# Dilated logits over 128 rows, with query halves moved by DMA, first steps a quarter of a unit later, and token factors spread by transposes

## The reference

```python
for g, (window, dil) in enumerate(((128, 1), (512, 4), (2048, 16))):
    s = einsum('bnqrhc,bnkrhc->bnrhqk', qb, kc) * HEAD_DIM ** -0.5    # 8 heads of 64
    logits = where(valid, s + bias, NEG_INF)
    m = max(logits); p = exp(logits - m); den = sum(p)
    num = einsum('bnrhqk,bnkrhc->bnqrhc', p, vc)
o = sum(num * exp(m - m_all)) / sum(den * exp(m - m_all))
```

## Time and profile before

| | us |
|---|---|
| median of 3 runs | 1864.54 (1863.68 to 1864.83) |
| the profiled execution | 1863.83 |
| its span | 1862.1 |
| TensorE busy | 1850.5 (99%) |
| VectorE busy | 1127.5 (61%) |
| ScalarE busy | 672.8 (36%) |
| GpSimd busy | 165.3 (9%) |

### The profile page before, as it was taken

One profiled execution on the slowest core, in us unless ns is written; L12 is line 12 of the kernel. 1 busy time (PEld: TensorE's weight loads), 2 busy tenths in 40 slices (PEclk: granted clock), 3 DMA queues, 4 the chain that ended last, 5 costly groups with the idle time before them and its releaser, 6 DMA issues.

```text
span 1862.1 us, 24221 instructions
## 1 busy us (share of the span) xinstructions
PE 1850.5 (99%) x8817; PEld 1535.1 (82%) x8817; DVE 1127.5 (61%) x1524; ACT 672.8 (36%) x975; POOL 165.3 (9%) x199
## 2 busy tenths in 40 slices
PE   9999999999999999999999999999999999999998
PEld 7888888888888888888888888888888878888887
DVE  7888788676676444686642354366776786325532
ACT  6323434343333333344321222225555653212221
POOL 0011112200000011002000000101211220000000
PEclk9999999999999999999999999999999999999999
DMA  4222222323233333223333343322222123333232
GB/s 161 81 89 80 80 68 80 113 91 101 90 101 94 109 103 125 84 75 93 119 101 93 115 121 97 104 93 71 78 69 80 47 90 113 102 93 100 90 102 68
DMA packets 55156, 175.29 MB, mean 94 GB/s; under 512 B 6201, under 2 KB 12857, under 8 KB 55074
## 3 DMA queue, kind: packets, MB, share of 16 engines
q1 hardware_dynamic: 49744, 170.43, 29.4%
q10 hardware_dynamic: 4818, 3.68, 0.9%
q0 software_dynamic: 512, 0.03, 0.0%
HBM read 171.96 MB, written 2.13 MB: 93 GB/s over the span
## 4 chain that ended last, share of the span: by engine, by line
PE 94%; DVE 5%; DMA 0%; issue 0%; ACT 0%; SPq 0%; DVEq 0%; ACTq 0%
PE ps L605 30%; PE ps L607 29%; PE ps L606 29%; PE ps L1101 1%; DVE wlo L1621 1%; PE ps L1132 1%; PE ps L1113 1%; PE ps L613 1%; PE ps L903 1%; PE ps L893 0%; DVE yr L1640 0%; DVE grm L1713 0%; PE ps L1144 0%; PE ps L980 0%; DVE h L2286 0%
## 5 line engine op out<-in xcount | busy, mean ns | idle before, releaser
L605 PE MATMUL ps<-xhi,whi 128*128 128x512 f32 x1568 | 617.2, 394 | 1.4 <-DVE wlo L1621 0.6
L607 PE MATMUL ps<-xlo,whi 128*128 128x512 f32 x1568 | 610.9, 390 | 0.0
L606 PE MATMUL ps<-xhi,wlo 128*128 128x512 f32 x1568 | 610.5, 389 | 0.0
L1621 DVE TENSOR_TENSOR wlo<-raw,whi 128x1024 fp32r<-128x1024 f32 x314 | 403.8, 1287 | 210.8 <-ACT whi L1257 210.6
L1257 ACT ACTIVATE whi<-raw 128x1024 fp32r<-128x1024 f32 x314 | 331.1, 1055 | 537.6 <-PE ps L607 475.4
L605 PEld LDWEIGHTS ps<-xhi,whi 128*128 128x128 f32 x1568 | 294.4, 188 | 64.9 <-DVE wlo L1621 1.9
L607 PEld LDWEIGHTS ps<-xlo,whi 128*128 128x128 f32 x1568 | 294.3, 188 | 62.0
L606 PEld LDWEIGHTS ps<-xhi,wlo 128*128 128x128 f32 x1568 | 294.6, 188 | 59.3
L605 PE MATMUL ps<-mh,whi 128*128 128x512 f32 (+1 forms) x528 | 202.2, 383 | 0.0
L606 PE MATMUL ps<-mh,wlo 128*128 128x512 f32 (+1 forms) x528 | 202.0, 383 | 0.0
L607 PE MATMUL ps<-mh,whi 128*128 128x512 f32 (+1 forms) x528 | 202.0, 383 | 0.0
(11 more groups left out here) (346 smaller groups left out, 1962.4 us busy)
## 6 DMA issues: line engine op xcount, KB each, us to landing
raw<-wst SPq DMA_DIRECT2D x314, 512.0 KB, 3.5
h<-xT SPq DMA_DIRECT2D x8, 256.0 KB, 5.6
out<-h SPq DMA_DIRECT2D x8, 256.0 KB, 2.2
raw<-wst SPq DMA_DIRECT2D x4, 256.0 KB, 5.4
bias_a<-bias_rows ACTq DMA_DIRECT2D x4, 256.0 KB, 4.6
bias_b<-bias_rows ACTq DMA_DIRECT2D x4, 256.0 KB, 4.4
wsf<-wsT ACTq DMA_DIRECT2D x1, 512.0 KB, 3.4
bsb<-bs ACTq DMA_DIRECT2D x1, 512.0 KB, 4.3
```

What stands on the lines that cost most here:

```text
L605: pe.matmul(o, w[0], x[0], start=first, stop=False, **kw)
L606: pe.matmul(o, w[1], x[0], start=False, stop=False, **kw)
L607: return pe.matmul(o, w[0], x[1], start=False, stop=done, **kw)
L1621: dve.tensor_tensor(wlo[:, n % SLOTS, :], raw[:, n % 2, :], whi[:, n % SLOTS, :].bitcast(F32), ALU.subtract).then_inc(s_split, 1)
```

## The change

The query and key parts of each group are laid out anew. `dqk[:, o, x]` holds, for head x, both halves of the query over 128 rows (high and low, one in each set of 64 rows), and `dqk[:, o, 2 + x]` holds the key's high part twice. One matmul over 128 rows then gives high by high plus low by high for a head; high by low (`dqk[:, o, 4]`) stays a pair over 64 rows. To lay this out, ScalarE copies the second head's high half within its rows (`head_halves`, at the second tick of the next unit), and issues two DMAs per q or k unit, 64 rows x 2 KB each, that move halves to the other rows; TensorE waits for the DMAs (`s_dqm`). Part 1 of the last pair keeps the old form. A burst now multiplies the 128-row products of both its steps first, then the 64-row ones. The steps of part 0 come one tick later, except the last two of pair 3, which keep theirs. The token factors are spread by transposes of the broadcast column.

```diff
--- before.py
+++ after.py
@@ -145,10 +145,11 @@
-    _d, _l = TICKS * (9 * _p + 6) - 1, TICKS * (9 * _p + 9)
+    _d, _l = TICKS * (9 * _p + 6), TICKS * (9 * _p + 9)
     for _s in range(4):
         _n = 8 * _p + _s
-        LOGITS_AT[_d + 3 * _s], TURN_AT[_d + 3 * _s + 2], SUMS_AT[_d + 3 * _s + 5] = _n, _n, _n
+        _t = _d + (3 * _s if _p < 3 else (0, 3, 5, 8)[_s])
+        LOGITS_AT[_t], TURN_AT[_t + 2], SUMS_AT[_t + 5] = _n, _n, _n
@@ -333,14 +334,15 @@
-            dqk = sb("dqk", [P, 3, 4, T], F32R, m)
+            dqk = sb("dqk", [P, 3, 5, T], F32R, m)
+            qlow = sb("qlow", [P, T], F32R, m)
...
+        def stacked(p, part):
+            return p < 3 or part == 0
+        def moves_before(p, o):
+            return 6 * p + 2 * o
...
@@ -962,8 +975,7 @@ spread()
-                        ins = pe.matmul(bank(7 - n)[:, t * P:(t + 1) * P], rtk[:, NT * n + t:NT * n + t + 1].to_broadcast([P, P]), ident,
-                                        start=t == 0, stop=True, skip_group_check=True)
+                        ins = pe.transpose(bank(7 - n)[:, t * P:(t + 1) * P], rtk[:, NT * n + t:NT * n + t + 1].to_broadcast([P, P]), ident)
@@ -1052,8 +1064,7 @@ last_spread(half)
-                    ins = pe.matmul(bank(6)[:, t * P:(t + 1) * P], rtok[:, t:t + 1].to_broadcast([P, P]), ident, start=t == tiles[0],
-                                    stop=True, skip_group_check=True)
+                    ins = pe.transpose(bank(6)[:, t * P:(t + 1) * P], rtok[:, t:t + 1].to_broadcast([P, P]), ident)
@@ -1082,25 +1093,47 @@
-            def logits(n):
+            def blocks_of(n):
...
-                for i, (o, q, k, c) in enumerate(blocks):
-                    for a, b in ((0, 2), (1, 2), (0, 3)):
-                        for x, r in enumerate(rows):
-                            ins = pe.matmul(logit_half(n)[:, x, c], dqk[r, o, a, q], dqk[r, o, b, k],
-                                            start=n % 2 == 0 and i == 0 and (a, b) == (0, 2), stop=b == 3, skip_group_check=True)
-                ins.then_inc(s_dlo, 1)
+            def logits(steps):
+                for n in steps:
+                    p, part, t = step_of(n)
+                    if n % 4 == 0:
+                        if stacked(p, part):
+                            pe.wait_ge(s_dqm, 32 * moves_before(p, 3 if part else 2))
+                        else:
+                            pe.wait_ge(s_dqk, 6 * p + 6)
+                    if n % 2 == 0 and n or n > PAIRED:
+                        pe.wait_ge(s_dlg, n)
+                for n in steps:
+                    p, part, t = step_of(n)
+                    for i, (o, q, k, c) in enumerate(blocks_of(n)):
+                        first = n % 2 == 0 and i == 0
+                        if stacked(p, part):
+                            for x in range(2):
+                                pe.matmul(logit_half(n)[:, x, c], dqk[:, o, x, q], dqk[:, o, 2 + x, k], start=first, stop=False,
+                                          skip_group_check=True)
+                        else:
+                            for qs in (dqk[:, o, 0, q], qlow[:, q]):
+                                for x, r in enumerate(HEAD_ROWS):
+                                    pe.matmul(logit_half(n)[:, x, c], qs[r, :], dqk[r, o, 2, k], start=first, stop=False,
+                                              skip_group_check=True)
+                                first = False
+                for n in steps:
+                    p, part, t = step_of(n)
+                    for o, q, k, c in blocks_of(n):
+                        for x, r in enumerate(HEAD_ROWS):
+                            ins = pe.matmul(logit_half(n)[:, x, c], dqk[r, o, x if stacked(p, part) else 0, q], dqk[r, o, 4, k],
+                                            start=False, stop=True, skip_group_check=True)
+                    ins.then_inc(s_dlo, 1)
@@ -1560,7 +1593,26 @@ ScalarE
+            def head_halves(k):
+                p, o, j = k // 9, k // 3 % 3, k % 3
+                if j == 2 or not stacked(p, o == 2):
+                    return
+                n = moves_before(p, o) + j
+                act.wait_ge(s_dqh, n + 1)
+                second = dqk[HEAD_ROWS[1], o, 2 * j + 1, :]
+                act.activation(second, dqk[HEAD_ROWS[1], o, 2 * j, :].bitcast(F32), ACT.Copy).then_inc(s_dqc, 1)
+                if n:
+                    act.wait_ge(s_dqm, 32 * n)
+                act.wait_ge(s_dqk, n + 1)
+                act.wait_ge(s_dqc, n + 1)
+                for r, a, src in ((HEAD_ROWS[0], 2 * j + 1, second if j else qlow[HEAD_ROWS[1], :]),
+                                  (HEAD_ROWS[1], 2 * j, dqk[HEAD_ROWS[0], o, 2, :] if j else qlow[HEAD_ROWS[0], :])):
+                    act.dma_start(dqk[r, o, a, :].bitcast(F32), src.bitcast(F32)).then_inc(s_dqm, 16)
             def attend(tick):
+                if tick % TICKS == 1 and 0 < tick // TICKS <= 36:
+                    head_halves(tick // TICKS - 1)
@@ -2142,7 +2194,13 @@ VectorE, out_of_bank(k)
-                split(dqk[:, o, 2 * j, :], dqk[:, o, 2 * j + 1, :], dst, s_dqk)
+                n = moves_before(p, o) + j
+                hi_, lo_ = dqk[:, o, 2 * j, :], dqk[:, o, 4, :] if j else qlow[:, :]
+                dve.tensor_copy(hi_, dst).then_inc(s_dqh, 1)
+                if j == 0 and n:
+                    dve.wait_ge(s_dqm, 32 * n)
+                dve.wait_ge(s_dqh, n + 1)
+                dve.tensor_tensor(lo_, dst, hi_.bitcast(F32), ALU.subtract).then_inc(s_dqk, 1)
```

More of the change, by code:

```diff
@@ L342, in build @@
             cAB = sb("cAB", [P, 4, NT, 4, 2], F32, m)
-            sb("behind_mlp", [P, 36 * T - 28 * T - 3 * NT * 4 * STATS - 6 * P - NT * 32], F32, m)
+            sb("behind_mlp", [P, 36 * T - 32 * T - 3 * NT * 4 * STATS - 6 * P - NT * 32], F32, m)
             with ExitStack() as m2:
@@ L562, in build @@
         s_dqk = sem("dilated_qk_split")
+        s_dqh = sem("dilated_qk_hi_done")
+        s_dqc = sem("dilated_qk_second_head_copied")
+        s_dqm = sem("dilated_qk_halves_moved")
         s_dtv = sem("dilated_v_transposed")
@@ L1094, in logits @@
                     k0 = (t - 1) * P if t else 0
-                    blocks = [(2, c, slice(k0, (t + 1) * P), slice(0 if t else P, 2 * P))]
-                else:
-                    blocks = [(o, slice((3 - t) * P, (4 - t) * P), slice(t * P, (t + 1) * P), slice(o * P, (o + 1) * P)) for o in range(2)]
-                for i, (o, q, k, c) in enumerate(blocks):
-                    for a, b in ((0, 2), (1, 2), (0, 3)):
-                        for x, r in enumerate(rows):
-                            ins = pe.matmul(logit_half(n)[:, x, c], dqk[r, o, a, q], dqk[r, o, b, k],
-                                            start=n % 2 == 0 and i == 0 and (a, b) == (0, 2), stop=b == 3, skip_group_check=True)
@@ L1103, in logits @@
-                ins.then_inc(s_dlo, 1)
+                    return [(2, c, slice(k0, (t + 1) * P), slice(0 if t else P, 2 * P))]
+                return [(o, slice((3 - t) * P, (4 - t) * P), slice(t * P, (t + 1) * P), slice(o * P, (o + 1) * P)) for o in range(2)]
+            def logits(steps):
[29 more added lines that the diff above has]
+                    ins.then_inc(s_dlo, 1)
@@ L1187, in attend @@
                     turned(TURN_AT[tick])
-                for n in MULTIPLIED_AT.get(tick, ()):
-                    logits(n)
+                if tick in MULTIPLIED_AT:
+                    logits(MULTIPLIED_AT[tick])
                 if tick in PART_AT:
```

## The result

The changed kernel takes 1878.80 us in the median of four runs (1876.76 to 1882.62), beside 1864.21 (1863.68 to 1864.83) for the kernel before on the same chip: ratio 1.0079, 95% interval 1.0067 to 1.0092, or +14.6 us. Forecast was +5.2 and 1869.3, with a range of 1861 to 1874. The direction was right, the size was not. The profiled execution took 1879.71. Of all executions told of here one, in experiment 5, ran at a mean granted clock of 0.752 and took 2311.9 us; it is no part of the ratios.

What follows compares the result with a forecast made beforehand. TensorE, busy 272.88 of 273 us in the dilated stage, was taken as the bound. Terms -1.3 + 0 + 0.3 + 2.25 + 1.5 + 1.4 + 1.1 = +5.2 gave 1869.0 profiled, 1869.3 as median; range 1861 to 1874.

Steps and rivals of the forecast that it cites:

- The form of the logits: Logits bursts in the dilated stage: 288 matmuls become 200 but slots stay 144, taken as 0 (bounds -5.5 to +1.3).
- The price of a slot: TensorE's logits: a stacked 128-row matmul of 128 columns costs 0.107 us, like a transpose; a pair pays it once.
- The spreads: Token factors by transposes: -0.85 us for eight spreads, -0.22 at each of the last norm's two; together -1.3.
- step 1's exponential: Second new wait: TensorE stalls before step 1's transposes, 0.7 us at p = 1 and 2, 0.1 at p=0; +1.5.
- the masking at p = 3: Last pair: the second logits pair keeps its old tick but waits for VectorE's masking; +1.4 us.
- the splits: Dilated stage: bursts cut differently by the later steps, seven splits at 0.05 us; +0.3 in all.
- Rival (a): The waits vanish, as slack or earlier landing hides most: 1863.8 to 1867.5 us, no change; chance 0.29.
- (c): Rival: the moves land like weights, 3.5 us from issue: 1873 to 1877 us; chance 0.12.
- First new wait: the moved halves: Logits at p = 1, 2, 3: TensorE waits 0.75 us each for ScalarE's two DMAs, +2.25; in time at p=0.
- Third: what follows: Steps 2 and 3 at p = 1 and 2: maskings and exponentials come late, 0.2 and 0.35 us per pair; +1.1.

Runs made afterwards that it cites:

- experiment 5: The kernel before, with ScalarE also making the copies and 44 DMAs into a spare tile that TensorE never waits for; 1864.65 us, ratio 1.0001.
- experiment 7: The kernel after with part 0's steps one more tick (1.36 us) later; 1865.43 us, ratio 1.0012.
- experiment 3: The kernel before with two 128-row matmuls and one 64-row pair per logits block, old ticks, no halves moved; 1864.88 us, ratio 1.0003.
- Experiment 2: The kernel before with only the later tick tables of the kernel after; 1868.09 us, ratio 1.0019.
- experiment 9: The kernel after, moves still issued, but TensorE waits only for VectorE's halves and reads only those; 1870.52 us, ratio 1.0034.
- experiment 1: The kernel before with only the token factors spread by transposes; 1863.28 us, ratio 0.9995.
- experiment 6: The kernel after with the second group's value split and the second merge factors' multiplication one tick later on VectorE; 1875.44 us, ratio 1.0058.

## Why the forecast was right and wrong

**Right.** The form of the logits costs nothing. Where nothing is waited for, the burst of two steps is this (TensorE's timeline, experiment 7, pair 1):

```profile
1319.46 0.39 PE L620 MATMUL ps<-xlo,whi 128*128 128x512 f32 x1
1319.68 1.00 PE L1122 MATMUL ps<-dqk 128*128 128x128 f32 x8
1320.62 0.66 PE L1134 MATMUL ps<-dqk 64*128 64x128 f32 x8
1321.21 0.50 PE L618 MATMUL ps<-xhi,whi 128*128 128x512 f32 x1
```

From the last dense start to the next it takes 1.75, for 1.81 before. The price of a slot, taken from the transposes, held (0.118 in experiment 3, forecast 0.107). That a slot is the time of a weight load is the forecast's inference; the runs show the price and not what sets it. The spreads were right (-1.4 in the trace for -1.3; -0.9 in the medians, inside their noise). So were step 1's exponential, 0.7 at p = 1 and 2 and 0.1 at p = 0, and the masking at p = 3, 1.4. Experiment 2 gives +3.9 for the +3.2 of these and the splits. Rival (a), that the waits vanish, did not come about. Nor did (c) where it was to decide: at the three long waits the second move landed after 2.5, 2.7 and 2.4 and not 3.5, and its 1873 to 1877 is below the time as well. Elsewhere 16 of 44 landed later than 3.5 (experiment 7).

**Wrong in size: "First new wait: the moved halves", +2.25.** TensorE's own waits came to 4.7, 2.4 more. At pair 1 the chain can be laid beside the forecast (VectorE's and ScalarE's timelines after):

```profile
1316.56 0.43 DVE L2199 CAST dqk<-mtmp 128x512 fp32r<-128x512 f32 x1
1317.02 0.69 DVE L2203 TENSOR_TENSOR dqk<-mtmp,dqk 128x512 fp32r<-128x512 f32 x1
```

```profile
1317.02 0.63 ACT L1604 ACTIVATE dqk<-dqk 64x512 fp32r<-64x512 f32 x1 [0.32 <-DVE dqk L2199]
1317.79 1.12 ACTq L1611 DMA_DIRECT2D dqk<-dqk  x2
```

All of it stands 0.74 later than in the earlier trace rows, and so does TensorE, so the stall compares: k_lo is done at 1317.71 and the logits start 3.08 behind it, where the forecast had 0.4 + 2.1 = 2.5. The copy took 0.63 for 0.60. The first issue began 0.08 behind k_lo and took 0.47 for the 0.37 of the earlier trace rows, and the second landed some 2.5 after its start for 2.1. The step that failed here is the price of a move: the issue and the landing were each taken short. Each of the three stalls was 1.3 to 1.5 for 0.75, and 0.6 more lay at p = 0 and at part 1's bursts, which the forecast had in time. The tile view of `dqk` gives the range of the durations (ns, min/median/max) and of the landings:

```profile
L1611 ACTq DMA_DIRECT2D dqk<-qlow x22: 468/574/623, 1234.8 to 1447.4; - x22
L1611 ACTq DMA_DIRECT2D dqk<-dqk x22: 468/546/887, 1238.2 to 1455.4; - x22
...
DMA to landing us min/median/max: 2.2/2.5/5.5
```

The median of 2.5 is that of q and k moves together. The page's 2.4 and 4.8 at the top are for the moves out of `qlow` and for those within `dqk`: 3 of 22 and 12 of 22 were issued together with a unit of weights.

**Wrong in size: "Third: what follows", +1.1.** Steps 2 and 3 waited 3.0 in sum, five times. The forecast named the mechanism, ScalarE's copies behind its issues, but priced it at one pair of issues, 0.74. It left out that the copy of the second head's half stands in front of them too: in the example of experiment 9 the copy takes 0.74 with the gap behind it and the two issues 1.1, and the copy of the probabilities comes 1.96 late.

**Missing: the clock.** The sum had no term for what TensorE does after a wait. The profile of before could not show it, since its clock is 1.00 throughout the stage and TensorE has no waits there; the forecast put six waits of 0.7 or more into that stage and bounded nothing behind them. It is 4.4 in the profiled execution.

The three together are 2.4 + 1.9 + 4.4 = 8.7 of the 10.7 us between the 1869.0 that the forecast had for the profiled execution and its 1879.71; the rest stands in no term. By the experiments: after less experiment 9 is 8.3 for TensorE's waits for the DMAs with what follows them, where starts give 4.7 for the waits and 3.0 for the two slow stretches behind them (the third, 1.4, stands behind the masking's wait), 7.7. Not settled is what decides whether a wait of 1 to 1.6 us is followed by a slow stretch. The kernel alone does not, as the clocks differ between executions of one kernel.

The only version below before in its median is experiment 1 (0.9 us, not told from nothing).

## What to carry to other kernels

Where TensorE is busy 99% of the time, fewer matmuls are no gain unless they are fewer slots in series (a 128-row matmul is one, and so is a pair of 64-row ones). A wait of 1 us or more that a change puts before TensorE is to be priced twice, alone and with a slow stretch of some 1.5 us behind it. Moves within SBUF need their time from the last producer to the consumer with both issues in it (here 3.1 us, and 2 to 3 more where a unit of weights is issued at the same time), and the engine that issues them should have nothing behind them that TensorE waits for: one tick more (1.36 us), which also let step 1's waits go, gave back 13.4 of 14.6 us.

## What was not expected of the hardware

- Waits of 1.1 to 1.4 us were at times followed by a stretch at 1.2 GHz (dense matmuls 0.427 apart for 0.227, seven in a row at pair 1), beginning within 2.3 us of the wait's end; four of four pauses of 2.07 us were, and one wait of 2.05 us was not. From one execution to the next of a kernel the number of such stretches changes (clocks of 0.996 to 0.999 in experiment 6).
- A DMA of 128 KB between 64 rows each, issued by ScalarE, occupied it for 0.47 to 0.62 us in most cases (0.89 once), where the issues of before were 0.37. It landed after 2.2 to 2.7 us, or after 4.7 to 5.5 when it was issued together with a unit of weights (15 of 15 in the kernel after; one of the other 29 took 3.8). The Trainium skill ("DMA: Bandwidth & Descriptors", "Anatomy of one DMA — SWDGE (gpsimd) path") fits 2.0 us plus the bytes over 436 GB/s on GpSimd's path, an estimate of 2.3 here: these moves go by ScalarE's queue, and the trace agrees for those that met no weights and not for the others.
- 44 such moves, 5.8 MB, beside the stream of weights cost nothing that can be measured where nothing waits for them (experiment 5, 0.9991 to 1.0011).
